# Score products of an attention stage issued in pairs on the two halves of TensorE's rows

## What is computed

```python
def swa_gqa_sinks(q, k, v, sinks, rel_bias):
    ...
    s = jnp.einsum('bcqhgd,bcshd->bchgqs', qc, kb) * (A_HEAD_DIM ** -0.5)
    ...
    s = jnp.where(valid[None, :, None, None], s + bias, -1e30)
    m = jnp.maximum(jnp.max(s, axis=-1, keepdims=True), sink)
    p = jnp.exp(s - m)
    denom = jnp.sum(p, axis=-1, keepdims=True) + jnp.exp(sink - m)
    o = jnp.einsum('bchgqs,bcshd->bcqhgd', p / denom, vb)

proj = (h @ w_in).astype(jnp.float32)
qa, ka, va, qb, kb, vb, gb = jnp.split(proj, list(np.cumsum(IN_SPLITS)[:-1]), axis=-1)
```

## Time and profile before

| | |
|---|---|
| median of 3 runs | 583.85 us (583.45 to 584.18) |
| profiled execution | 581.58 us |
| its span in the trace | 579.9 us |
| TensorE busy | 555.3 us, 96% of the span |
| VectorE, ScalarE, GpSimd busy | 424.4, 358.0 and 116.2 us |
| chain that ended last | TensorE 85% |

### The profile page before, as it was taken

How to read it: one execution, slowest core, us unless ns; L and a number is a source line. 1 busy time by engine, 2 the same in 40 slices (tenths; PEclk the granted TensorE clock), 3 DMA queues, 4 the chain that set the end, 5 groups by cost and what they waited for, 6 DMA issues and landing times.

```text
span 579.9 us, 8103 instructions
## 1 busy us (share of the span) xinstructions
PE 555.3 (96%) x2782; PEld 456.2 (79%) x2783; DVE 424.4 (73%) x580; ACT 358.0 (62%) x475; POOL 116.2 (20%) x102
## 2 busy tenths in 40 slices
PE   4999999999999999998999999999999999999991
PEld 3988888888877888876788888888888888888860
DVE  3663467544674853467998898888998888988886
ACT  5563454683133444234888787888877888777733
POOL 3250000000000000002442334423344323411100
PEclk9999999999999999999999999999999999999997
DMA  8999112202120135686999999999999999998073
GB/s 297 375 271 388 49 36 73 73 0 76 72 72 1 49 134 193 242 290 210 353 387 374 372 364 362 388 347 354 365 358 382 371 368 375 360 389 323 24 291 145
DMA packets 72045, 144.33 MB, mean 249 GB/s; under 512 B 3794, under 2 KB 13322, under 8 KB 71888
## 3 DMA queue, kind: packets, MB, share of 16 engines
q1 hardware_dynamic: 65936, 124.96, 61.2%
q0 software_dynamic: 6080, 19.00, 9.5%
HBM read 132.77 MB, written 14.69 MB: 254 GB/s over the span
## 4 chain that ended last, share of the span: by engine, by line
PE 85%; DVE 5%; DMA 4%; issue 2%; ACT 1%; SPq 1%; POOL 0%; POOLq 0%; DVEq 0%
PE ps L1317 24%; PE ps L1319 23%; PE ps L1318 23%; PE ps L1324 6%; PE ps L1429 2%; PE ps L1399 2%; DMA arena<-y_dram 2%; PE ps L1466 2%; PE ps L1454 1%; PE ps L1497 1%; PE ps L1420 1%; DMA arena<-norm_g 1%; DMA arena<-h_dram,meta 1%; PE ps L1337 1%; DVE act_lo L911 1%
## 5 line engine op out<-in xcount | busy, mean ns | idle before, releaser
L1117 DVE TENSOR_TENSOR lo_ring<-arena,hi_ring 128x2048 fp32r<-128x2048 f32 x94 | 215.1, 2291 | 28.5 <-ACT hi_ring L804 27.5
L1317 PE MATMUL ps<-hi_ring,act_hi 128*128 128x512 f32 x576 | 232.6, 404 | 0.5 <-DVE act_lo L911 0.5
L1319 PE MATMUL ps<-hi_ring,act_lo 128*128 128x512 f32 x576 | 225.2, 391 | 0.0
L1318 PE MATMUL ps<-lo_ring,act_hi 128*128 128x512 f32 x576 | 224.6, 390 | 0.0
L804 ACT ACTIVATE hi_ring<-arena 128x2048 fp32r<-128x2048 f32 x94 | 180.2, 1917 | 18.7 <-PE ps L1319 18.7
L1317 PEld LDWEIGHTS ps<-hi_ring,act_hi 128*128 128x128 f32 x576 | 108.2, 188 | 27.3 <-issue 6.0
L1319 PEld LDWEIGHTS ps<-hi_ring,act_lo 128*128 128x128 f32 x576 | 108.1, 188 | 23.6
L1318 PEld LDWEIGHTS ps<-lo_ring,act_hi 128*128 128x128 f32 x576 | 108.5, 188 | 20.2
L911 DVE TENSOR_TENSOR act_lo<-ps,act_hi 128x512 fp32r<-128x512 f32 x64 | 41.7, 683 | 11.2 <-ACT act_hi L669 5.3
L901 DVE SCALAR_TENSOR_TENSOR lo_ring<-arena,over,hi_ring 128x512 fp32r<-128x512 f32 x32 | 23.6, 748 | 32.8 <-ACT hi_ring L640 32.8
L563 POOL DMA_INDIRECT y_dram<-y,row_info x15 | 16.1, 1074 | 149.7 <-issue 149.7
(11 more groups left out here) (197 smaller groups left out, 579.0 us busy)
## 6 DMA issues: line engine op xcount, KB each, us to landing
arena<-w_gate SPq DMA_DIRECT2D x32, 1024.0 KB, 15.5
arena<-w_up SPq DMA_DIRECT2D x32, 1024.0 KB, 15.9
arena<-w_down SPq DMA_DIRECT2D x32, 1024.0 KB, 15.5
arena<-w_in SPq DMA_DIRECT2D x16, 512.0 KB, 10.8
y_dram<-arena POOLq DMA_DIRECT2D x8, 512.0 KB, 12.2
arena<-w_out SPq DMA_DIRECT2D x4, 1024.0 KB, 5.1
arena<-y_dram SPq DMA_DIRECT2D x8, 512.0 KB, 6.7
arena<-w_in SPq DMA_DIRECT2D x3, 1024.0 KB, 13.1
```

Of the source, the lines that this page charges most:

```text
L1117: nc.vector.tensor_tensor(lo(N1 + n12), raw(n12), hi(N1 + n12).bitcast(F32), ALU.subtract).then_inc(lo_done, 1)
L1317: nc.tensor.matmul(dst, a_hi, b_hi, start=start, stop=False)
L1318: nc.tensor.matmul(dst, a_hi, b_lo, start=False, stop=False)
L1319: return nc.tensor.matmul(dst, a_lo, b_hi, start=False, stop=stop)
```

## The change

Query heads keep their natural order: heads `2j` and `2j + 1` lie on the two halves of the rows of chunk `j`. The keys are kept a second time, in `ka_s`, with the two halves exchanged, which takes two more copies on ScalarE. Within a unit the products now go to rows 0 to 63, 64 to 127, 0 to 63, 64 to 127, and those of the two halves write to different banks. `scores` and `turn_v` wait for 8 copies. VectorE reads the scores with a view that puts each head where it belongs.

```diff
+O_KS = O_SCM + 704
...
+        ka_s = region(O_KS, 512)
...
+        prob_pairs = region(O_P, 1024).rearrange("p (i a j) -> p a i j", i=2, a=2)
+        bias_pairs = region(O_BIAS, A_HEADS * WIN).rearrange("p (i a j) -> p a i j", i=4, a=2)
...
-            views = raw_of(g)[:, c], hi(g)[:, c], lo(g)[:, c]
-            if g >= 2:
-                return views
-            return (views[0].rearrange("p (a j c) -> p j a c", a=2, j=4),
-                    *(v.rearrange("p (j a c) -> p j a c", a=2, j=4) for v in views[1:]))
+            return raw_of(g)[:, c], hi(g)[:, c], lo(g)[:, c]
...
                     nc.scalar.copy(ka_t if t == 1 else v_t, ps[:, 4 + t // 2, :]).then_inc(qkv_copied, 1)
+                    if t == 1:
+                        for a in range(2):
+                            nc.scalar.copy(ka_s[(1 - a) * A_DIM:(2 - a) * A_DIM, :],
+                                           ps[a * A_DIM:(a + 1) * A_DIM, 4, :]).then_inc(qkv_copied, 1)
...
-                    elif g < 2:
-                        for a in range(2):
-                            ins = nc.vector.scalar_tensor_tensor(dst[:, :, a, :], src[:, :, a, :], gain,
-                                                                 src_hi[:, :, a, :].bitcast(F32), ALU.mult, ALU.subtract)
...
-                        prob[:, 2 * half:2 * half + 2, CHUNK + j0:], sc[:, :, j0:], A_DIM ** -0.5,
-                        bias[:, 4 * kv + 2 * half:4 * kv + 2 * half + 2, j0:], ALU.mult, ALU.add)
+                        prob_pairs[:, half, :, CHUNK + j0:], sc[:, :, j0:], A_DIM ** -0.5,
+                        bias_pairs[:, half, 2 * kv:2 * kv + 2, j0:], ALU.mult, ALU.add)
...
-                pe.wait_ge(qkv_copied, 6)
+                pe.wait_ge(qkv_copied, 8)
...
-                rows = slice(kv * A_DIM, (kv + 1) * A_DIM)
                 keys = slice(t * P - CHUNK + j0, (t + 1) * P)
                 for hh in range(4):
-                    c = (hh % 2) * WIN
-                    ins = nc.tensor.matmul(ps[:, 4 + hh // 2, c + j0:c + WIN], qa_t[rows, hh, t * P:(t + 1) * P],
-                                           ka_t[rows, keys], start=True, stop=True)
+                    a, c = hh % 2, (hh // 2) * WIN
+                    rows = slice(a * A_DIM, (a + 1) * A_DIM)
+                    ins = nc.tensor.matmul(ps[:, 4 + a, c + j0:c + WIN], qa_t[rows, 2 * kv + hh // 2, t * P:(t + 1) * P],
+                                           (ka_t if a == kv else ka_s)[rows, keys], start=True, stop=True)
...
             def turn_v():
...
-                pe.wait_ge(qkv_copied, 6)
+                pe.wait_ge(qkv_copied, 8)
```

## The result

The changed kernel takes 576.23 us (median of 4 runs, 575.17 to 576.67) against 583.65 us of the kernel before measured beside it: a ratio of 0.9858, with a 95% interval of 0.9832 to 0.9884. That is 7.4 us less; the prediction had 2.1 us less, 581.8 us from 583.85. The profiled execution takes 576.34 us, its span is 574.2 us.

What follows compares the result with a forecast made beforehand. TensorE's own instructions, busy 96% of the span, were taken to bound the kernel. Score products 1.94 plus split 0.15 gave 2.1 us off, other terms 0: 581.8 us from 583.85, range 579.9 to 583.9.

Steps and rivals of the forecast that it cites:

- the value taken for the score products: Attention's score units on TensorE: halves overlap in streaming but not in loads, saving 1.94 us; whole forecast's chance 0.42.
- Matmuls start in order: Score products on TensorE: assumed to start in program order across both halves, part of the 1.94 us saving.
- the four-step case: Score units: each pair of products takes the time of one, 4.85 us saved with the start, 579.0 us; chance 0.06.
- Weight loads go one at a time: Score products on TensorE: each load takes 0.107 us and none overlap, so units of 128 keys save nothing.
- full overlap with five steps: Score units: loads of different halves also overlap, 3.55 us saved, 580.1 us with the start; chance 0.26 including four steps' 0.06.
- Split of blocks 0 and 1: Near 20 us at the start: eight pieces become one instruction each, shortening TensorE's wait; 0.15 us saved.
- Copies and the wait for 8: Before the values' copy: ScalarE's 3.62 us idle time takes in two copies of at most 1.2 us; cost 0 us.
- The wait at 76 us and VectorE behind the scores: Attention: TensorE's 1.0 us wait on VectorE's chain stays, both sides come forward together, and VectorE's logits change by 0.
- Slower by a drain at each change of half: Score units: 24 changes of half at 0.2 us each lose 4.8 us, less 0.15, giving 588.5 us; chance 0.10.
- adding 2.3 us: Whole kernel: the runs' median of 583.85 us lies 2.3 us above the profiled execution, so 579.5 becomes 581.8 us.

Runs made afterwards that it cites:

- grouped order: Changed kernel with a unit's score products issued low, low, high, high half instead of low, high, low, high: 579.7 us (10 runs), ratio 0.9921.
- 16 matmuls in turn: Changed kernel with each score product issued twice, low, high, low, high, 16 instructions a unit: 585.16 us in one execution.
- the two repetitions: The changed kernel measured twice more, unchanged, against the kernel before: 578.45 us (6 runs), ratio 0.9894, and 578.36 us (7 runs), ratio 0.9890.
- second profiled execution: From the control, the kernel before once more, unchanged: 583.01 us (12 runs), ratio 0.9977; its profiled execution took 584.86 us.
- 16 grouped: Changed kernel with each score product issued twice, the four low-half ones first, then the four high-half ones: 589.03 us in one execution.
- 4.85 us for 32: Changed kernel with each score product issued four times, eight low-half ones first, then eight high-half ones: 609.74 us in one execution.
- Quarters: Changed kernel with scores in products of 64 rows by 64 columns, each 64 queries meeting 128 keys, in two orders: 578.46 us (0.9897) and 578.26 us (0.9906).

## Why the prediction was wrong

The step that failed is the value taken for the score products: "halves stream at the same time, matmuls start in order, those of one half follow each other, and weight loads go one at a time". It gave 0.32 us a unit of 192 and nothing for 128, 1.94 us in all. The chain shows 0.64 us less a unit of 192 and 0.43 less for 128, 4.7 us in all. The runs showed the first and third part right and the two others wrong:

- *Matmuls start in order.* They do not, across halves. In the grouped order the fifth matmul starts with the first. In turn, too, an order kept to would leave five steps, and four are measured. The order argument is what had made me give the four-step case only 0.06: A1 A2 B1 B2 seemed to leave A1 and B2 alone.
- *Weight loads go one at a time.* Loads of the two halves go side by side: the 8 loads of a unit of 128 keys pass in 0.43 us, which is 0.054 us each. The 0.108 us a load that the earlier trace rows show for full-height products, and that the prediction took for all, is no floor for two halves together. Whether it is one within a half stays open, as 128 columns take 0.108 us to stream.

With both corrected it is the four-step rival of the prediction: 4 x 0.161 x 6 + 4 x 0.108 x 2 = 4.7 us. The chain shows 5 x 0.64 + 0.63 + 2 x 0.43 = 4.7 us less in the units, and the stretch 4.5 us less; the tile products behind the units gave back some 0.2 us. (By its own terms the rival's sum is 4.88 us with the start, not 4.85, and full overlap with five steps is 580.1 us, while the stated range begins at 579.9.) That rival was also the one for which the Trainium skill spoke ("TensorE: Matmul & The Clock Gate", Part 3). Its rule that a pack takes about the time of one matmul agrees with the traces, where a pair takes one step of 0.161 us. The Trainium skill's rule in "TensorEngine Tiling (Array Packing)", Key Properties, that a change of tile within a mode does not drain, is borne out by the traces too: 16 matmuls in turn take 1.50 us. What I weighed against that rival, rows of full-height products, said nothing on two halves at work with different weights. The Trainium skill's "TensorE: Matmul & The Clock Gate", Part 3, also has matmuls start strictly in the order of the program; the grouped run contradicts that across halves.

The other terms:

- *Split of blocks 0 and 1*, 0.15 us: right, 0.12 us in the wait and 0.2 us up to the first score product.
- *Copies and the wait for 8*, 0 us: right, by after and by the run with the copies alone.
- *The wait at 76 us and VectorE behind the scores*: right, a wait of 1.03 us, and VectorE still idles 1.37 us.
- *Slower by a drain at each change of half*: out, since a unit's order in turn has four steps and the same 0.2 us around them.

With 4.7 and 0.15 us the sum would have been 579.0, a ratio of 0.9917. The three measurements of after are 576.2, 578.5 and 578.4. The intervals of the two repetitions hold 0.9917 (they lie 5.1 and 5.8 us under the kernel before beside them), and that of the first measurement, 0.9832 to 0.9884, does not.

What made the first four executions some 2.2 us shorter than the repetitions is known in part. Between traces, the clock behind the gather makes up to 2.8 us and the end behind the last write 32.4 to 34.9 us. The mean granted clock over the whole span was 0.995 or 0.996 in all four of the first, the traced one with its full clock behind the gather among them, and 0.988 to 0.993 in six of the thirteen others. But two of those others took 579.3 and 579.5 us at 0.995. So the clock is one cause, argued and not shown for these four, and it is not the only one. The prediction also put the profiled span on the median by adding 2.3 us, as if a constant lay between them. The traces of the kernel before make it scatter: its second profiled execution lies above the median, at 584.86 us.

## What to carry to other kernels

Products of 64 rows that follow each other on one half of the array run one after another. Put them on both halves and their steps halve, weight loads included (a unit went from 1.49 to 0.85 us), which can be worth a second copy of an operand on an engine that idles. In all runs here the two halves wrote to different banks; whether they must was not tested. Issue them in turn: one half may overtake some four matmuls of the other, but with longer groups the gain comes only once, at the border. And where the trace shows a resource only in one mode, its pace there is no bound for another: give the rival that speaks of the other mode a larger chance than 0.06.

## What was not expected of the hardware

- The high half overtook four matmuls and four loads of the low half (0.86 us for 8, grouped), but not eight: 2.25 us for 16 grouped, 4.85 us for 32, a saving of about three steps of 0.161 in both.
- Loads of weights for different halves go side by side: 8 of 128 columns in 0.43 us of a unit, where full-height ones take 0.108 us each.
- Quarters work the same with float32: 16 instructions of 64 rows, 64 columns and 128 moving columns in 0.60 us.
- Entering and leaving the 64-row form costs the same 0.4 us in all versions. The work between is now 0.64 or 0.43 us.
- The mean clock behind a wait of 2.2 to 3.0 us for the gathered rows was 1.00, 0.95 or 0.90 over the window from 255 to 290 us, and the wait's length did not decide which: 2.4 us came before 1.00 in before and before 0.90 in the second repetition of after.
